# Gathering the second expert table by used experts, with four places for tiles and three for rows

## The chip, the cores and the metric

The kernel runs on one core of one Trainium2 chip. The metric is the device time of the whole program in microseconds (us). TensorE is the matrix engine, VectorE (DVE) and ScalarE (ACT) the elementwise ones, GpSimd (POOL) issues the indirect DMAs through the software queue, SyncE (SP) issues the plain DMAs through a hardware queue.

## What is computed

A trunk of two layers over 256 tokens of width 2048. Each layer has four parallel mixers (Fourier, S5, attention, RWKV-7), a projection, and then a product-key expert layer ("PEER"). Only the last matters here, cut to its core:

```python
def peer_ffn(h, w_query, sub_keys, expert_u, expert_v):   # 8 heads, 128 x 128 = 16384 experts, top 16 a head
    q = (xc @ w_query).reshape(PEER_CHUNK, PEER_HEADS, 2, PEER_HALF)
    sc = jnp.einsum('chpd,hpkd->chpk', q, sub_keys)
    s1, i1 = lax.top_k(sc[:, :, 0], PEER_TOPK)
    s2, i2 = lax.top_k(sc[:, :, 1], PEER_TOPK)
    ...
    top_s, pos = lax.top_k(cand_s, PEER_TOPK)
    idx = jnp.take_along_axis(cand_i, pos, axis=-1)
    gate = jax.nn.softmax(top_s, axis=-1)
    u = jnp.take(expert_u, idx, axis=0)
    act = jax.nn.gelu(jnp.einsum('chkd,cd->chk', u, xc), approximate=False)
    vsel = jnp.take(expert_v, idx, axis=0)
    return jnp.einsum('chk,chkd->cd', (gate * act), vsel)
```

Each token picks 8 x 16 = 128 experts of 16384; each expert has one row of 2048 floats (8 KB) in each of two tables, `peer_u` and `peer_v`. All is float32.

## The kernel before

`build` runs a loop over the two layers; each iteration runs `mixers`, `rwkv`, `route` and `experts`. The change lies in `experts`, and in what `build` hands to it.

`experts` splits the 256 tokens. The first 160 (`DENSE`) go through the tables as a whole, in tiles: tile i holds the 128 experts with first key i, 1 MB. In the first stage TensorE multiplies each tile of the first table with the tokens (`tile(j)`, 16 products of 128x128 by 128x160, L1674, 32 matmul records), ScalarE applies GELU into `W[:, j, :]`. From tile `FIRST` = 64 on, `one_hot` and `gates` build, in 40 groups of 4 tokens, the matrix of gate weights by expert (L1683), and VectorE multiplies it into `W` (L1992 for tiles that are done, L1995 for the current one). After tile 127 `W[e, i, n]` is, for each of the 16384 experts and 160 tokens, gate times GELU, and it is exactly 0 where token n didn't pick the expert. In the second stage TensorE multiplies each tile of the second table by `W[:, j, :]` into six banks that hold the sum over all 128 tiles (L1747).

The other 96 tokens go by rows, in three sets of 32 (`SETS`). A "row" is one step: for 128 pairs of token and pick (one a partition) the row of the table is gathered. 32 steps on the first table give dot products, 32 on the second a weighted sum, so a layer has 192 row steps (`ROWS_IN`). GpSimd issues two gathers a step, one for each half of the row (L1631, 4 KB pieces for 128 partitions), into `place`, a ring of `RING` = 4 places, after `place_free` says that the step `RING` before is served. `serve(n)` on VectorE waits for the step's own DMA semaphore and runs one operation of 128x2048 (L1937 for the first table, L1943 for the second, L1940 for the first step of a sum). `served(j)` says how many steps stand in VectorE's order before tile j is over: 30 up to tile 63, then nine for ten tiles, 87 at tile 127; the other 105 follow freely during the second stage. The widened tokens of a set (`widen`, four groups of four transposes, L1697), and the folds of a set's sum into the output (`fold`, four single products, L1710, then `fold_add` on VectorE) stand at fixed tiles of TensorE's order: `WIDEN_0`, `WIDEN_1`, `FOLD_0` in the first stage, `WIDEN_2` = 36 and `FOLD_1` = 80 in the second. The third fold comes after the last tile.

Table tiles go through `ring`, `SLOTS` = 3 places of 1 MB. SP issues all 256 tile loads of a layer in order, each after `tile_mm` says that the tile `SLOTS` before it is multiplied (L1595 for the first table, L1600 for the second). TensorE waits on a semaphore of the place, `tile_in[slot]`. All orders are written by hand; nothing is planned at run time.

## Time and profile before

| | |
|---|---|
| median of three runs | 4014.94 us (4009.41 to 4017.21) |
| the profiled execution's own time | 4015.24 us |
| its span, first to last instruction | 4013.4 us |
| mean granted TensorE clock | 0.974 of full speed |
| TensorE busy (matmul / weight load) | 94% / 85% |
| VectorE, ScalarE, GpSimd busy | 57%, 11%, 24% |
| bytes moved by DMA | 1077.47 MB |

The expert part of a layer takes some 1200 us: in the first layer from 778 to 1986 us of the span, in the second from 2778 to 3988 us. A row of the profile has the line, engine, operation, what it writes and reads, how many, the busy time with the mean of one, and the idle time of the engine before it with what ended that. Matmul records overlap, since matmuls are pipelined, so a group's length counts and not the duration of one.

### The profile page before, as it was taken

The numbers are of one execution on the slowest core, as the hardware profiler recorded it, in microseconds if no ns is written. First come the engines' busy times: TensorE is split into PE (matmuls) and PEld (weight loads), VectorE is DVE, ScalarE is ACT, GpSimd is POOL, SyncE is SP. The second block draws the span as 40 slices with busy tenths as digits, with TensorE's granted clock in tenths as the row PEclk, the third lists the DMA queues.
The fourth block names the chain that finished last, engine by engine and source line by source line (L and its number), as shares of the span: only waits on it lengthen the run. The fifth ranks groups of instructions, "written<-read, shape, count | busy, mean of one in ns | idle before, by whom it ended". The sixth has DMA issues, their size and how long they took to land. (4 is left out here: it accounts for less than half of the span.)

```text
span 4013.4 us, 63920 instructions
## 1 busy us (share of the span) xinstructions
PE 3753.4 (94%) x26660; PEld 3401.8 (85%) x26660; DVE 2291.9 (57%) x4099; ACT 429.4 (11%) x1020; POOL 964.7 (24%) x868
## 2 busy tenths in 40 slices
PE   6997889999999999999879978899999999999997
PEld 5786774899999999999767867748999999999997
DVE  5965742785287544443469657517853875444434
ACT  1022210100111000000010232101001110000000
POOL 2610000034033333333225100000341333333331
PEclk9997899999999999999989978999999999999999
DMA  5430015399799999999744300154997999999997
GB/s 156 136 116 10 2 43 162 126 372 401 290 384 382 415 415 415 414 413 414 305 133 130 116 10 1 43 162 142 379 404 288 382 385 415 415 415 415 413 413 302
DMA packets 334770, 1077.47 MB, mean 268 GB/s; under 512 B 52196, under 2 KB 150872, under 8 KB 268440
## 3 DMA queue, kind: packets, MB, share of 16 engines
q1 hardware_dynamic: 223896, 670.72, 44.0%
q0 software_dynamic: 110592, 402.70, 25.3%
q8 instruction: 212, 3.47, 0.4%
q14 instruction: 70, 0.57, 0.0%
HBM read 1071.23 MB, written 2.10 MB: 267 GB/s over the span
## 5 line engine op out<-in xcount | busy, mean ns | idle before, releaser
L1747 PE MATMUL bank<-ex_W,ex_tile 128*128 128x160 f32 x8192 | 1132.3, 300 | 38.8 <-DMA ex_tile<-in_peer_v 38.8
L1747 PEld LDWEIGHTS bank<-ex_W,ex_tile 128*128 128x128 f32 x8192 | 1114.9, 190 | 59.7 <-DMA ex_tile<-in_peer_v 53.0
L1674 PE MATMUL bank<-ycT,ex_tile 128*128 128x160 f32 x8192 | 1140.2, 300 | 20.3 <-DMA ex_tile<-in_peer_uT 19.9
L1674 PEld LDWEIGHTS bank<-ycT,ex_tile 128*128 128x128 f32 x8192 | 1116.9, 190 | 36.0 <-DMA ex_tile<-in_peer_uT 30.4
L1631 POOL DMA_INDIRECT ex_row<-in_peer_u,ex_rows x384 | 403.5, 1051 | 1852.7 <-DVE ex_rows L1907 1187.4
L1943 DVE SCALAR_TENSOR_TENSOR ex_sums<-ex_row,ex_weight,ex_sums 128x2048 f32<-128x2048 f32 x186 | 436.9, 2349 | 412.9 <-DMA ex_row<-in_peer_v,ex_rows 412.8
L1937 DVE CUSTOM_DVE_ANT_0 ex_row<-ex_row,ex_h_wide 128x2048 f32<-128x2048 f32 x192 | 438.5, 2290 | 363.7 <-DMA ex_row<-in_peer_u,ex_rows 362.4
L1631 POOL DMA_INDIRECT ex_row<-in_peer_v,ex_rows x384 | 363.7, 947 | 878.9 <-DVE ex_sums L1943 565.7
L359 PE MATMUL pj_bank<-pj_hT,pj_piece 128*128 128x256 f32 x2048 | 458.7, 383 | 5.6 <-DMA pj_piece<-in_w_in 3.8
L359 PEld LDWEIGHTS pj_bank<-pj_hT,pj_piece 128*128 128x128 f32 x2048 | 387.9, 191 | 71.5 <-issue 13.8
L826 PE MATMUL bank<-arena,ycT 128*128 128x512 f32 x512 | 222.4, 593 | 2.0 <-PEq L911 2.0
L826 PEld LDWEIGHTS bank<-arena,ycT 128*128 128x128 f32 x512 | 96.6, 190 | 121.4 <-issue 121.2
L996 PE MATMUL bank<-arena 128*128 128x128 f32 x1152 | 140.7, 283 | 7.6 <-DVE arena L1344 7.5
L996 PEld LDWEIGHTS bank<-arena 128*128 128x128 f32 x1152 | 136.5, 198 | 10.3 <-issue 10.1
L1995 DVE TENSOR_TENSOR ex_W<-ex_W,ex_gelu 128x160 f32<-128x160 f32 (+26 forms) x128 | 35.2, 275 | 182.2 <-ACT ex_gelu L1791 113.8
L1419 PE MATMUL bank<-ycT,query_w 128*128 128x256 f32 x512 | 114.9, 382 | 2.0 <-PEq L1436 2.0
L1793 ACT ACTIVATE ex_W<-bank 128x160 f32<-128x160 f32 (+20 forms) x206 | 56.9, 276 | 518.4 <-PE bank L1674 518.4
L1419 PEld LDWEIGHTS bank<-ycT,query_w 128*128 128x128 f32 x512 | 95.8, 190 | 16.5 <-issue 2.7
L1921 DVE TENSOR_SCALAR ex_hot<-consts,ex_picksT 128x128 f32<-128x128 f32 x320 | 109.1, 341 | 0.0
L1518 DVE TENSOR_TENSOR x<-bank,x 128x512 f32<-128x512 f32 x16 | 11.1, 692 | 168.3 <-PE bank L826 168.1
L1920 DVE TENSOR_SCALAR ex_hot<-consts,ex_picksT 128x128 f32<-128x128 f32 x320 | 90.1, 282 | 15.4 <-ACT ex_picksT L1825 15.4
L607 POOL TENSOR_TENSOR s_table<-s_factor 128x1024 f32<-128x1024 f32 x16 | 30.8, 1927 | 268.7 <-DVE s_factor L712 153.1
(375 smaller groups left out, 3107.0 us busy)
## 6 DMA issues: line engine op xcount, KB each, us to landing
ex_tile<-in_peer_uT SPq DMA_DIRECT2D x256, 1024.0 KB, 8.1
ex_tile<-in_peer_v SPq DMA_DIRECT2D x256, 1024.0 KB, 8.2
pj_piece<-in_w_in SPq DMA_DIRECT2D x32, 2048.0 KB, 8.8
arena<-in_w_out SPq DMA_DIRECT2D x16, 2048.0 KB, 8.1
query_w<-in_peer_w_query SPq DMA_DIRECT2D x16, 1024.0 KB, 5.8
ex_row<-in_peer_u,ex_rows POOLq DMA_INDIRECT x384, 13.0
ex_row<-in_peer_v,ex_rows POOLq DMA_INDIRECT x384, 12.4
x<-in_x SPq DMA_DIRECT2D x1, 2048.0 KB, 8.9
```

What stands on the lines that cost most here:

```text
L359: mm = mmul(pj_bank[:, n % 2, m * SEQ:m * SEQ + SEQ], piece[:, n % 2, k, m * P:m * P + P], hT[:, k, :], start=(m == 0 and k == 0), stop=(k ...
L826: mm = nc.tensor.matmul(bank[:, out_bank(n) + b, :], ycT[:, kh * HALF_K + k, b * P:b * P + P], out_w["place"][:, i % 2, k, :], start=(kh = ...
L996: mm = mmul(bank[:, b, j * P:j * P + P], left[:, d, j, :], right[:, d, j, :], start=(j == 0), stop=True, skip_group_check=True)
L1419: mm = nc.tensor.matmul(bank[:, h % 2, 0:SEQ], query["w"][:, h % WRING, k, :], hT[k // 4][:, k % 4, :], start=(k == 0), stop=(k == KT - 1) ...
L1631: nc.gpsimd.indirect_dma_start(out=place[:, n % RING, half * D // 2:(half + 1) * D // 2], out_offset=None, in_=tables[table][:, :], in_off ...
L1674: mm = mmul(o, ring[:, j % SLOTS, k * P:k * P + P], hT[k // 4][:, k % 4, 0:DENSE], start=(k == 0), stop=(k == KT - 1))
L1747: mm = mmul(bank[:, at_, lo:lo + DENSE], ring[:, i % SLOTS, m * P:m * P + P], W[:, j, :], start=(j == 0 and m % 3 == 0), stop=(j == TILES ...
L1793: last = A.activation(W[:, j, n:DENSE], a[:, n:DENSE], ACT.Gelu)
L1920: V.tensor_scalar(hot2[:, g % 2, i, :], c("iota"), picksT[:, 1, n:n + 1], None, ALU.is_equal)
L1921: mm = V.tensor_scalar(hot1[:, g % 2, i, :], c("iota"), picksT[:, 0, n:n + 1], picksT[:, 2, n:n + 1], ALU.is_equal, ALU.mult)
L1937: V.tensor_tensor_reduce(out=row, in0=row, in1=h_wide[:], scale=1.0, scalar=0.0, op0=ALU.mult, op1=ALU.add, accum_out=dot[:, step:step + 1 ...
L1943: V.scalar_tensor_tensor(sums[:], row, weight[:, step:step + 1], sums[:], ALU.mult, ALU.add)\
```

## The change

The tiles of the second table are no longer loaded whole by SP. VectorE works out an index for each expert (`want`, for eight tiles at a time, `CHUNK`): the largest absolute value of `W` over the 160 tokens, a comparison with 0 that gives 65536 where it is 0, and an addition of the expert's number (`expert`: key times 128 plus partition plus the layer's base). GpSimd issues one indirect gather a tile (`v_tile`), 128 indices, 8 KB pieces; an index beyond the last expert is out of bounds and is skipped, so the place keeps what it had, which is multiplied by a `W` of 0. The first 13 chunks' indices are made in VectorE's order after tiles 104 to 116, the last three after tile 127. GpSimd's order is now written out: rows up to `rows_ahead(0)` = 86, then for each tile of the second table its gather and, until the 192 are out, one row step (two gathers). The ring of tiles has four places, that of rows three. TensorE waits for a second-table tile on a new semaphore a place, `v_in`, whose value goes on over the layers, so it is compared with a value that depends on the layer. The fixed tiles of `widen(2)` and `fold(1)` move from 36 to 28 and from 80 to 64, and the row before which `fold_add(1)` starts from 152 to 149.

```diff
--- before.py
+++ after.py
@@ -33,8 +33,8 @@
 HALF_K = 8
 WRING = 3
 TILES = KEYS
-SLOTS = 3
-RING = 4
+SLOTS = 4
+RING = 3
 SET, SETS, STEPS = 32, 3, 32
 DENSE = SEQ - SET * SETS
 ROWS_IN = SETS * 2 * STEPS
@@ -43,7 +43,7 @@
 FIRST = 64
 BEFORE = 30
 WIDEN_0, EXPS_1, WIDEN_1, FOLD_0 = 2, 16, 90, 114
-WIDEN_2, FOLD_1, FOLD_1_AT = 36, 80, 152
+WIDEN_2, FOLD_1, FOLD_1_AT = 28, 64, 149
 A_BANKS = (4, 5, 3)
 G_BANKS = (0, 1, 2)
 OUT_BANKS = (0, 1, 2, 3, 4, 5)
@@ -92,6 +92,7 @@
     parts["fold"] = (p % SET) == np.arange(SET)[None, :]
     parts["even"] = (p // S5C) % 2 == 0
     parts["odd"] = (p // S5C) % 2 == 1
+    parts["lane"] = p
     parts["eps"] = np.full((P, 1), NORM_EPS)
     parts["eps_kk"] = np.full((P, 1), 1e-12)
     parts["eps_gn"] = np.full((P, 1), 64e-5)
@@ -167,6 +168,7 @@
 
 
         row_in = [sem(f"row_in{i}") for i in range(RING)]
+        v_in = [sem(f"v_in{i}") for i in range(SLOTS)]
         kept = len(first_sem)
         with nc.Fori(0, DEPTH) as layer:
             rw = ExitStack()
@@ -193,7 +195,7 @@
                      "rms": sb(rw, "rms", [P, 3, TB]), "w_in": [sem(f"query_in{i}") for i in range(WRING)]}
             hT = [ycT[:, 4 * g:4 * g + 4] for g in range(4)]
             route(nc, t, layer, sem, sb, bank, c, col, x, ycT, hT, query, out_w)
-            experts(nc, t, layer, sem, sb, bank, c, x, hT, query, W, low, layer_base, row_in)
+            experts(nc, t, layer, sem, sb, bank, c, x, hT, query, W, low, layer_base, row_in, v_in)
             rw.close()
             with nc.Block() as block:
                 @block.sync
@@ -1524,12 +1526,24 @@
                 do(V.reciprocal(rms[:, 2], rms[:, 1]))
 
 
+NOWHERE = 65536.0
+CHUNK = 8
+
+
+def rows_ahead(j):
+
+    return min(served(TILES - SLOTS - 1) + RING - 1 + j, ROWS_IN)
+
+
 def served(j):
 
     return BEFORE + max(j - FIRST + 1, 0) * 9 // 10
 
 
-def experts(nc, t, layer, sem, sb, bank, c, x, hT, query, W, low, layer_base, row_in):
+def experts(nc, t, layer, sem, sb, bank, c, x, hT, query, W, low, layer_base, row_in, v_in):
+
+
+
 
 
 
@@ -1546,6 +1560,7 @@
                                                                                       "gates_times", "tile_times")]
     four_ready, rows_ready, place_free, dots_ready, gelu_ready, sums_ready = [sem("ex_" + n) for n in ("four", "rows", "place_free", "dots",
                                                                                           "gelu", "sums")]
+    index_ready = sem("ex_index")
     wide_mm, wide_out, fold_mm, fold_added = [sem("ex_" + n) for n in ("wide_mm", "wide_out", "fold_mm", "fold_added")]
     out_mm, out_out, back_mm, x_added, dve_own = [sem("ex_" + n) for n in ("out_mm", "out_out", "back_mm", "x_added", "dve")]
     with ExitStack() as st:
@@ -1566,6 +1581,8 @@
         picksT = sb(st, "ex_picksT", [P, 3, DENSE])
         rows = sb(st, "ex_rows", [P, SETS, 2, STEPS], U32)
         half_on = sb(st, "ex_half_on", [P, 1])
+        weighty, expert = sb(st, "ex_weighty", [P, TILES]), sb(st, "ex_expert", [P, TILES])
+        wanted = sb(st, "ex_wanted", [P, TILES], U32)
         share_w = sb(st, "ex_share", [P, SETS, STEPS])
         dot, dot_gelu = sb(st, "ex_dot", [P, STEPS]), sb(st, "ex_dot_gelu", [P, STEPS])
         weight = sb(st, "ex_weight", [P, STEPS])
@@ -1585,6 +1602,7 @@
         best = nc.alloc_sbuf_tensor_at("ex_best", [P, TB, PEER_H, TOPK], F32, offset=before_hot + 3072)
         outT = W[:, 0:KT, :]
         tables = [t[n].rearrange("l e (h d) -> (l e h) d", h=2) for n in ("peer_u", "peer_v")]
+        v_rows = t["peer_v"].rearrange("l e d -> (l e) d")
 
         with nc.Block() as block:
             @block.sync
@@ -1593,11 +1611,6 @@
                     if free is not None:
                         sp.wait_ge(tile_mm, free)
                     sp.dma_start(ring[:, slot, :], t["peer_uT"][layer, i].rearrange("p k e -> p (k e)"))\
-                        .then_inc(tile_in[slot], 16)
-
-                def v_tile(i, slot, free):
-                    sp.wait_ge(tile_mm, free)
-                    sp.dma_start(ring[:, slot, :], t["peer_v"].rearrange("l (i e) d -> l i e d", e=KEYS)[layer, i])\
                         .then_inc(tile_in[slot], 16)
 
                 for h in range(WRING, PEER_H):
@@ -1611,19 +1624,10 @@
                         u_tile(lap * SLOTS + e, e, lap * SLOTS + (e + 1 - SLOTS))
                 for i in range(whole_laps * SLOTS, TILES):
                     u_tile(i, i % SLOTS, i + 1 - SLOTS)
-                ahead = SLOTS - TILES % SLOTS
-                for i in range(ahead):
-                    v_tile(i, (TILES + i) % SLOTS, TILES + i + 1 - SLOTS)
-                with sp.Fori(0, (TILES - ahead) // SLOTS) as lap:
-                    for e in range(SLOTS):
-                        v_tile(lap * SLOTS + (ahead + e), e, lap * SLOTS + (TILES + ahead + e + 1 - SLOTS))
-                for i in range(ahead + (TILES - ahead) // SLOTS * SLOTS, TILES):
-                    v_tile(i, (TILES + i) % SLOTS, TILES + i + 1 - SLOTS)
 
             @block.gpsimd
             def _(pool):
-                pool.wait_ge(rows_ready, SETS * 4 * 2)
-                for n in range(ROWS_IN):
+                def gather(n):
                     s, table, step = n // (2 * STEPS), n // STEPS % 2, n % STEPS
                     if n >= RING:
                         pool.wait_ge(place_free, n - RING + 1)
@@ -1633,6 +1637,24 @@
                             in_=tables[table][:, :],
                             in_offset=bass.IndirectOffsetOnAxis(ap=rows[:, s, half, step:step + 1], axis=0))\
                             .then_inc(row_in[n % RING], 16)
+
+                def v_tile(j):
+                    slot = (TILES + j) % SLOTS
+                    if j % CHUNK == 0:
+                        pool.wait_ge(index_ready, j // CHUNK + 1)
+                    pool.wait_ge(tile_mm, TILES + j + 1 - SLOTS)
+                    nc.gpsimd.indirect_dma_start(
+                        out=ring[:, slot, :], out_offset=None, in_=v_rows[:, :],
+                        in_offset=bass.IndirectOffsetOnAxis(ap=wanted[:, j:j + 1], axis=0),
+                        bounds_check=DEPTH * EXPERTS - 1, oob_is_err=False).then_inc(v_in[slot], 16)
+
+                pool.wait_ge(rows_ready, SETS * 4 * 2)
+                for n in range(rows_ahead(0)):
+                    gather(n)
+                for j in range(TILES):
+                    v_tile(j)
+                    for n in range(rows_ahead(j), rows_ahead(j + 1)):
+                        gather(n)
 
             @block.tensor
             def _(pe):
@@ -1733,7 +1755,7 @@
                 pe.wait_ge(gates_times, GROUPS)
                 for j in range(TILES):
                     i = TILES + j
-                    pe.wait_ge(tile_in[i % SLOTS], 16 * (i // SLOTS + 1))
+                    pe.wait_ge(v_in[i % SLOTS], layer * (16 * ((TILES - 1 - j % SLOTS) // SLOTS + 1)) + 16 * (j // SLOTS + 1))
                     if j >= FIRST:
                         pe.wait_ge(tile_times, j - FIRST + 1)
                     if 0 <= j - WIDEN_2 < 4:
@@ -1922,6 +1944,15 @@
                                              picksT[:, 2, n:n + 1], ALU.is_equal, ALU.mult)
                     mm.then_inc(hot_ready, 1)
 
+                def want(i):
+
+                    some = slice(CHUNK * i, CHUNK * i + CHUNK)
+                    dve.wait_ge(gates_times, GROUPS)
+                    dve.wait_ge(tile_times, max(CHUNK * i + CHUNK - FIRST, 1))
+                    do(V.tensor_reduce(weighty[:, some], W[:, some, :], AX.X, ALU.max, apply_absolute_value=True))
+                    do(V.tensor_scalar(weighty[:, some], weighty[:, some], 0.0, NOWHERE, ALU.is_equal, ALU.mult))
+                    V.tensor_tensor(wanted[:, some], weighty[:, some], expert[:, some], ALU.add).then_inc(index_ready, 1)
+
                 def serve(n):
                     s, table, step = n // (2 * STEPS), n // STEPS % 2, n % STEPS
                     row = place[:, n % RING, :]
@@ -1976,6 +2007,9 @@
                     serve(n)
                 share(0)
 
+                do(V.tensor_scalar(expert[:], c("iota"), float(KEYS), c("lane"), ALU.mult, ALU.add))
+                do(V.tensor_scalar(expert[:], expert[:], layer_base[:], None, ALU.add))
+
                 dve.wait_ge(picks_out, 1)
                 one_hot(0)
                 one_hot(1)
@@ -1997,6 +2031,10 @@
                         one_hot(g + 2)
                     for n in range(served(j - 1), served(j)):
                         serve(n)
+                    if 0 <= g - GROUPS < (FIRST + GROUPS) // CHUNK:
+                        want(g - GROUPS)
+                for i in range((FIRST + GROUPS) // CHUNK, TILES // CHUNK):
+                    want(i)
                 for n in range(served(TILES - 1), ROWS_IN):
                     if n - FOLD_1_AT in (0, 2, 4, 6):
                         fold_add(1, (n - FOLD_1_AT) // 2)
```

## Rows read from the trace of the kernel before

**Rows 1.** The page, parts 1 and 2: busy time; GB/s in 40 slices.
```profile
PE 3753.4 (94%) x26660; PEld 3401.8 (85%) x26660; DVE 2291.9 (57%) x4099; ACT 429.4 (11%) x1020; POOL 964.7 (24%) x868
...
GB/s 156 136 116 10 2 43 162 126 372 401 290 384 382 415 415 415 414 413 414 305 133 130 116 10 1 43 162 142 379 404 288 382 385 415 415 415 415 413 413 302
```

**Rows 2.** Stages: us, PE, PEld, DVE, ACT, POOL busy, PEclk, DMA share, GB/s.
```profile
778.20:1060.60 282.40, 274.95 (x2002) 271.76 (x2001) 171.16 (x461) 30.77 (x78) 81.18 (x68) 1.00 0.90 354
1061.85:1276.20 214.35, 214.35 (x1637) 214.35 (x1637) 172.87 (x433) 31.61 (x127) 61.90 (x66) 1.00 0.93 356
1282.00:1394.66 112.66, 110.20 (x778) 105.09 (x777) 56.95 (x70) 7.29 (x24) 39.33 (x42) 1.00 1.02 414
1394.66:1986.10 591.44, 571.06 (x4122) 559.47 (x4120) 247.87 (x155) 7.61 (x16) 195.95 (x205) 1.00 1.01 410
3396.30:3987.70 591.40, 570.34 (x4116) 558.68 (x4114) 248.09 (x155) 7.22 (x15) 195.51 (x205) 1.00 1.01 410
```

**Rows 3.** TensorE in order of time: start us, us, what [idle before, releaser].
```profile
787.00 0.60 PE L1697 MATMUL bank<-consts,ex_four 128*128 128x128 f32 x4
787.43 4.51 PE L1674 MATMUL bank<-ycT,ex_tile 128*128 128x160 f32 x32
791.78 0.60 PE L1697 MATMUL bank<-consts,ex_four 128*128 128x128 f32 x4
...
1276.75 1.05 PE L1683 MATMUL bank<-ex_hot 128*128 128x128 f32 x8
1277.64 2.61 PE L1674 MATMUL bank<-ycT,ex_tile 128*128 128x160 f32 x18
...
1772.69 1.04 PE L1710 MATMUL bank<-ex_sums,consts 128*32 128x512 f32 x2
1773.67 2.58 PE L1747 MATMUL bank<-ex_W,ex_tile 128*128 128x160 f32 x17
```

**Rows 4.** The page, costliest groups: TensorE's tile products, busy and idle before.
```profile
L1747 PE MATMUL bank<-ex_W,ex_tile 128*128 128x160 f32 x8192 | 1132.3, 300 | 38.8 <-DMA ex_tile<-in_peer_v 38.8
...
L1674 PE MATMUL bank<-ycT,ex_tile 128*128 128x160 f32 x8192 | 1140.2, 300 | 20.3 <-DMA ex_tile<-in_peer_uT 19.9
```

**Rows 5.** Tile loads, issue to landing: u-tiles of 800 to 1000, v-tiles of 1400 to 1980.
```profile
DMA to landing us min/median/max: 4.7/8.2/9.8
...
DMA to landing us min/median/max: 7.8/8.2/9.5
```

**Rows 6.** Row gathers, to landing: 800 to 1000, 1100 to 1270, 1276 to 1394, 1400 to 1980.
```profile
DMA to landing us min/median/max: 4.5/11.2/19.4
...
DMA to landing us min/median/max: 6.8/8.1/11.4
...
DMA to landing us min/median/max: 6.3/12.2/18.2
...
DMA to landing us min/median/max: 8.7/15.7/21.8
```

**Rows 7.** GpSimd in order of time, v-stage: the two gathers of one row step.
```profile
1402.31 0.94 POOL L1631 DMA_INDIRECT ex_row<-in_peer_u,ex_rows  x1 [2.12 <-DVE ex_dot L1937]
1403.55 0.94 POOL L1631 DMA_INDIRECT ex_row<-in_peer_u,ex_rows  x1 [0.30 <-issue]
```

**Rows 8.** VectorE in order of time; then a reduction's group (busy us, mean ns).
```profile
1300.58 0.32 DVE L1995 TENSOR_TENSOR ex_W<-ex_W,ex_gelu 128x160 f32<-128x160 f32 x1 [1.81 <-ACT ex_gelu L1791]
...
1457.31 2.35 DVE L1943 SCALAR_TENSOR_TENSOR ex_sums<-ex_row,ex_weight,ex_sums 128x2048 f32<-128x2048 f32 x1 [5.63 <-DMA ex_row<-in_peer_v,ex_rows]
...
1981.80 4.85 DVE L1943 SCALAR_TENSOR_TENSOR ex_sums<-ex_row,ex_weight,ex_sums 128x2048 f32<-128x2048 f32 x2 [2.60 <-DMA ex_row<-in_peer_v,ex_rows]
...
L1882 DVE TENSOR_REDUCE ex_picks<-ex_match 128x32 f32<-128x512 f32 x32 | 21.9, 686 | 1.1
```

**Rows 9.** Waits of 778 to 1060.6: total us, times, longest.
```profile
DVE ex_row L1937 <- DMA ex_row<-in_peer_u,ex_rows: 49.4, 14, 6.9
DVE ex_total L1892 <- ACT ex_picks L1798: 48.0, 1, 48.0
```

## The prediction

> **What bounds the kernel now.** I read the page's first two parts, then the busy time by stage, then TensorE's order of time, then landings and waits. TensorE is busy for 94% of the span, and through the expert part of each layer DMA moves 380 to 415 GB/s in most slices [rows 1]. So two limits lie close together, and the stages must be priced one by one [rows 2]. I name them by table tile: "u-tiles" are the 128 of the first table, "v-tiles" the 128 of the second.
>
> TensorE's own pace [rows 3]: a tile is 32 matmul records; one starts at 787.43 and the group behind it at 791.78, so a tile is 4.35 us (the record of 4.51 holds the last matmul's tail, 0.16 us). A fold matmul adds 0.98 us (1773.67 - 1772.69), a group of four widening transposes 0.43 us (787.43 - 787.00), a gate group 0.89 us (1277.64 - 1276.75).
>
> Without any stall the stages of one layer would be:
> - u-tiles 0 to 61, 778.20 to 1060.60: 62 x 4.35 + 4 x 0.43 = 271.5 us, measured 282.4: 10.9 us of stall.
> - u-tiles 62 to 103 with the gates: 42 x 4.35 + 40 x 0.89 + 4 x 0.43 + 1.3 for the picks' transposes = 221.4 us; from 1060.60 to the end of tile 103 (1277.64 + 4.35 = 1282.0) it took 221.4. TensorE alone sets it.
> - u-tiles 104 to 127, 1282.00 to 1394.66: 24 x 4.35 + 4 x 0.98 = 108.3, measured 112.7: 4.4 us of stall.
> - v-tiles, 1394.66 to 1986.10: 128 x 4.35 + 4 x 0.98 + 4 x 0.43 = 563, measured 591.4, and 591.4 again in the second layer: 28 us of stall.
>
> The stalls end with an ex_tile transfer: 38.8 us of idle TensorE before v-tiles and 20.3 before u-tiles over both layers [rows 4] (the row counts less than I do, since each stall also lays bare a tail). In the v-stage DMA is at 410 GB/s. One MB-unit (1.05 MB, a full tile or a row pair for 128 partitions) at 410 to 415 GB/s costs 2.53 to 2.56 us, and 128 tiles plus 105 rows are 233 units, 590 to 596 us: the v-stage is exactly DMA-bound. Everything that the change can give there is 28 us a layer, not the time of the bytes it saves.
>
> **Part 1: bytes.** Which experts are used follows from the reference on its own inputs: I ran its top-k and marked, for the first 160 tokens (those that go through tiles), each expert that is picked. It leaves 11323 of 16384 in layer 0 (69.1%) and 11254 in layer 1 (68.7%), 53 to 118 of 128 in a tile. Skipping the rest saves 0.31 x 128 = 40 units a layer, 101 us of DMA time; the load falls to 193 units, 491 us. The average is under TensorE's 563 us.
>
> **Part 2: pacing.** The new program issues one row gather behind each v-tile until all 192 are out: 86 are out before the first v-tile, so 106 v-tiles carry a row, and 22 carry none. While rows run, a tile period asks 1.69 units, 4.27 to 4.33 us, against 4.35: 98% of TensorE's pace. This is an average over engines and tiles. A tile lands only when its slowest DMA engine is done. Taking eight partitions for an engine, the busiest eight (of consecutive ones) hold 75% in layer 0 and 73% in layer 1. Summed over windows of tiles, with the larger of 4.35 and the busiest eight's time at 2.53 us a unit, the mean period is 4.89 us if nothing evens out, 4.64 for windows of four tiles, 4.55 for eight, 4.47 for sixteen. There are four places for tiles and three for rows, so four to eight is what can even out; I take 4.6. The v-stage is then 106 x 4.6 + 22 x 4.35 = 583, and 2 us for that part of folds and widening that falls where TensorE is the later one: 585, 6 us less than 591.4. Ends: 563 (all hidden, -28) and, at 4.89, 614 + 6 = 620 (+29).
>
> The Trainium skill ("DMA: Bandwidth & Descriptors", The descriptor swizzle) gives the eight partitions of an engine in another order than mine, 0 to 3 with 32 to 35 and so on. Counted so, the busiest engine of layer 0 holds 78% of its rows and windows of four and eight give 4.63 and 4.55; the sum is the same by either, and no row here shows which engine serves which partition.
>
> **Part 3: GpSimd.** SP's v-tile loads, with nothing behind them on SP's queue, become gathers. A gather of 128 pieces takes 0.94 us and the next starts 1.24 us after it [rows 7]. Three a period are 3.72 us, within 4.6. A tile's pieces are 8 KB where rows' are 4 KB, and no row shows the cost of such an instruction: between 0.94 (one index, one piece; I take it, as the row is of 128 indices too) and twice that, 4.66 us a period. The queue is in order: v-tile j waits for tile j-4 to be multiplied, and the row gather behind it for its place; whichever waits holds the other. For the v-tile the cover is three tiles, 13.1 us.
>
> **Part 4: three row places.** A place's cycle is: second half issued 1.24 us after the first, landing, served in 2.35 us, 0.3 us to GpSimd's restart [rows 6, 7, 8]. At a landing of 8.1 us (gate stretch, DMA 93% busy) that is 12.0 us, 4.0 a row; at 15.7 us (v-stage of before, saturated) 19.6 us, 6.5 a row. At the 4.6 us I take, landing may be 9.9 us; I hold that it is near the 8.1 row, since 1.69 units in 4.6 us are 93% busy too. In the u-stage the gates stretch needs a row per 5.8 us: hidden. For tiles 104 to 127, landing 12.2 us gives 5.4 us a row, times 0.9 rows a tile 4.8 us a tile, against 4.7 now: 0 to 2 us a layer. Before tile 60 VectorE waits 49.4 us for rows and then 48.0 us for the softmax's exponentials [rows 9], which ScalarE makes only at tile 60: 30 rows, each 1.3 us later ((11.2 + 3.9) x (1/3 - 1/4) us, from the median landing there [rows 6]), use 38 us of that 48. Cost 0.
>
> **Part 5: four tile places.** A u-tile lands 8.2 us after issue, up to 9.8 [rows 5], and three places cover two tiles, 8.7 us: that is where the 10.9 us of stall come from, while DMA is at 90%. Four places cover 13.1 us, beyond every landing seen. I give back 9 of 10.9 us, bounds 0 and 10.9. In tiles 104 to 127 one more tile is there when the stretch begins and the first v-tile is only 0.69 units: DMA work falls from 44 units (22 u-tiles, a v-tile, 21 rows) to 42 (20, 0.69, 21), 106 us and under the 108.3. I take 3 of 4.4 us, bounds 0 and 4.4, and 1 us back for rows and for the next part.
>
> **Part 6: the index work.** Per 8 tiles one reduction of 128x1280 and two tiny operations. A 128x512 reduction takes 0.686 us [rows 8], so 1280 elements take at most 2.5 times that, 1.7, and the two others no more than the 0.32 of a 128x160 product each: 2.3 us at most, 16 times. The first 13 stand in tiles 104 to 116, where VectorE idles 1.81 us or more before each product [rows 8]; the serving and the product of the next tile are queued behind them. Cost 0 to 2 us, in the 1 us above. The last three run before v-tile 104 needs them. TensorE's waits now compare with a layer-dependent value: 0 to 0.07 us a tile, two serves back to back with such a wait take 4.85 us where each takes 2.35 [rows 8], 0.07 beside each; taken 0, since matmuls run unbroken over the present waits.
>
> **Sum.** Per layer -6 (v-stage) - 9 - 3 + 1 (u-stage) = -17, twice -34. The profiled execution had 4015.24 us (span 4013.4 and 1.8 around it), 0.3 from the median 4014.94. Forecast 4015 - 34 = 3981 us.
>
> **Rivals.** (a) The row and tile chains even out fully and the v-stage nears TensorE's floor: period 4.4 to 4.5, v-stage -17 to -28, total 3937 to 3962. For it: average demand 98%. Against: a tile with over 92 used experts asks, with its row, more than 4.35 us, and 49 and 53 of 128 in the two layers have more.
>
> (b) Slower: the shared queue. Now the v-tile lands in 8.2 us while a row beside it needs 15.7 [rows 5, 6]: a tile on SP's queue has a lead over what GpSimd's queue holds. In the new kernel v-tile and rows stand in GpSimd's queue, so the tile loses that lead, and three places for rows throttle GpSimd, which then issues the next v-tile late. It decides from a period of (602 - 98) / 106 = 4.75 us, where the v-stage loses the 11 us that the u-stage gives. At 4.9 us, a row landing of 10.8: v-stage 617, total 4015 + 2 x (26 - 11) = 4045. A doubled issue cost of the tile gathers (4.66 us and waits) ends there too. The Trainium skill ("DMA: Bandwidth & Descriptors", Queues, rings and completion order) says an engine takes turns between rings by packet; the landings above agree with it.
>
> (c) The skip saves nothing (an index beyond the bound still moves a piece): 2 units a period, 5.06 us, v-stage 106 x 5.06 + 98 = 634, total 4015 + 2 x (43 - 11) = 4079.
>
> (d) The gains and (b) cancel: period 4.7 to 4.8, 4007 to 4023.
>
> **Chances.** Forecast (3962 to 4006) 0.44, (a) 0.15, (d) 0.15, (b) 0.20 (4023 to 4070), (c) 0.06. Faster by over 0.2% (8 us, about what a measurement tells from no change) 0.59, within 0.15, slower 0.26. Range 3945 to 4050: it cuts the tips of (a) and (b), and (c).
>
> **What would show it.** Right: the bytes read fall by 80 units, 84 MB, the v-stage is 575 to 590 us, landings of rows there near 10 us, idle before u-tiles falls from 20 us to under 5. Wrong: GpSimd's v-tile gathers take near 2 us; bytes not lower; TensorE's wait for v-tiles grows; VectorE waits more before rows in tiles 104 to 127. The weakest step is the period of 4.6 us: 0.1 us there is 21 us in the total.

## The result, and the profile after

The changed kernel takes 4116.31 us (median of 4 runs, 4106.81 to 4123.07), the kernel before 4016.07 beside it: ratio 1.0251, 95% interval 1.0226 to 1.0275. It is 2.5% slower. The forecast, 3981 us in a range up to 4050, was wrong, in sign too. The profiled execution of after has 4114.04 us, span 4112.2.

The page of after, parts 1 and 2 (answering [rows 1]), then groups of its part 5 (answering [rows 4, 7]; in each, after the bar: busy time and mean ns of one, then the idle time before them and its releaser):

```profile
PE 3786.5 (92%) x26660; PEld 3428.7 (83%) x26660; DVE 2350.2 (57%) x4199; ACT 429.4 (10%) x1020; POOL 1501.8 (37%) x1124
GB/s 152 133 113 10 1 61 140 186 391 414 311 383 390 337 337 336 347 341 328 131 129 129 113 10 1 63 140 204 393 412 310 374 389 357 341 337 343 337 320 125
DMA packets 334774, 994.07 MB, mean 242 GB/s; under 512 B 62385, under 2 KB 161061, under 8 KB 278629
...
L1769 PE MATMUL bank<-ex_W,ex_tile 128*128 128x160 f32 x8192 | 1170.3, 305 | 111.1 <-DMA ex_tile<-in_peer_v,ex_wanted 110.1
...
L1696 PE MATMUL bank<-ycT,ex_tile 128*128 128x160 f32 x8192 | 1132.3, 300 | 0.0
...
L1635 POOL DMA_INDIRECT ex_row<-in_peer_v,ex_rows x384 | 471.8, 1229 | 435.5 <-DVE ex_sums L1974 207.2
...
L1646 POOL DMA_INDIRECT ex_tile<-in_peer_v,ex_wanted x256 | 377.3, 1474 | 194.4 <-PE bank L1769 128.2
```

Three things stand here. The bytes fell as worked out. The idle time before u-tiles is gone (20.3 us before). The idle time before v-tiles went from 38.8 to 111.1 us although DMA there moves only some 340 GB/s, and the mean of GpSimd's gathers, 1.23 and 1.47 us, is no longer near the 0.94 on which the sum rested. (A gather is one indirect DMA that GpSimd issues; its mean is GpSimd's busy time for one.)

By stages, for both kernels (us, layer 1 / layer 2; the stages are those of [rows 2]):

| | u-tiles 0–61 | 62–103 | 104–127 | v-stage |
|---|---|---|---|---|
| before | 282.4 / 282.6 | 221.4 | 112.7 / 113.1 | 591.5 / 592.3 |
| forecast | 273.4 | 221.4 | 110.7 | 585 |
| after | 271.4 / 271.3 | 221.4 | 118.6 / 116.2 | 648.4 / 648.6 |

The spans differ by 98.8 us: v-stages +56.9 +56.3, early u-tiles -11.0 -11.3, late u-tiles +5.9 +3.1, and 1 less in the rest. (Some expectations below count 645 us for this stage, or a period of 5.14 us; the stages of the table give 648.5 and 5.19.) Busy time of each engine by stretch in after (columns: stretch and length, PE, PEld, DVE, ACT, POOL, each with its count, then the granted clock, DMA's busy share and GB/s): tiles 104 to 127, the v-stage of layer 1, that part of it in which rows run, the v-stage of layer 2.

```profile
1271.90:1390.60 118.70, 111.04 (x779) 106.14 (x778) 79.62 (x109) 7.29 (x24) 40.97 (x41) 0.97 0.96 378
1390.60:2039.00 648.40, 590.75 (x4122) 572.05 (x4122) 253.84 (x164) 7.65 (x16) 468.33 (x336) 0.98 0.87 313
1390.60:1935.00 544.40, 487.25 (x3365) 469.20 (x3365) 249.14 (x162) 5.17 (x11) 444.79 (x315) 0.98 0.93 338
3438.90:4087.50 648.60, 590.18 (x4123) 571.92 (x4122) 253.57 (x164) 7.60 (x16) 468.75 (x336) 0.98 0.86 312
```

In the 544.4 us with rows GpSimd is busy for 444.79 in 315 gathers, and each gather has 0.30 us ahead of it: 445 + 95 = 540 us. GpSimd has no time left. TensorE is busy for only 487 us of the stretch, and DMA moves 338 GB/s where before it moved 410. GpSimd's order of time in after, and below it VectorE's over the same microseconds (start, duration, engine, line, operation; in brackets the idle time before it and its releaser):

```profile
1501.40 1.00 POOL L1646 DMA_INDIRECT ex_tile<-in_peer_v,ex_wanted  x1 [0.30 <-issue]
1502.70 0.94 POOL L1635 DMA_INDIRECT ex_row<-in_peer_v,ex_rows  x1 [0.30 <-issue]
1503.94 2.38 POOL L1635 DMA_INDIRECT ex_row<-in_peer_v,ex_rows  x1 [0.30 <-issue]
1506.63 0.99 POOL L1646 DMA_INDIRECT ex_tile<-in_peer_v,ex_wanted  x1 [0.31 <-issue]
1507.93 1.85 POOL L1635 DMA_INDIRECT ex_row<-in_peer_v,ex_rows  x1 [0.30 <-issue]
1510.08 0.94 POOL L1635 DMA_INDIRECT ex_row<-in_peer_v,ex_rows  x1 [0.30 <-issue]
1511.33 3.11 POOL L1646 DMA_INDIRECT ex_tile<-in_peer_v,ex_wanted  x1 [0.31 <-issue]
```
```profile
1503.16 2.35 DVE L1974 SCALAR_TENSOR_TENSOR ex_sums<-ex_row,ex_weight,ex_sums 128x2048 f32<-128x2048 f32 x1 [4.12 <-DMA ex_row<-in_peer_v,ex_rows]
1506.61 2.35 DVE L1974 SCALAR_TENSOR_TENSOR ex_sums<-ex_row,ex_weight,ex_sums 128x2048 f32<-128x2048 f32 x1 [1.10 <-DMA ex_row<-in_peer_v,ex_rows]
1511.21 2.35 DVE L1974 SCALAR_TENSOR_TENSOR ex_sums<-ex_row,ex_weight,ex_sums 128x2048 f32<-128x2048 f32 x1 [2.25 <-DMA ex_row<-in_peer_v,ex_rows]
```

A tile gather takes 1.00 us, not 1.88, so the larger pieces are not the cost. But a gather that begins while VectorE passes over a row ends 0.8 to 0.9 us after that pass: 1505.51 + 0.81 = 1506.32, 1508.96 + 0.82 = 1509.78, 1513.56 + 0.88 = 1514.44. It happens to row and tile gathers alike. Below this is called the hold. The gather at 1506.63 isn't held: it begins 0.02 us behind the start of its pass, so what starts first seems to go first. Between 1400 and 1900 us there are 289 gathers, three for each of 96 v-tiles. Of these 105 begin inside a pass. Ten of the 105 begin in the first 0.1 us of it and take their usual time, and 95 are held and take 2.36 us on average. The 184 that begin outside a pass take 0.94 (median). One in three, 1.4 us longer: 3 x 1.26 + 1.4 x 95 / 96 = 5.17 us a v-tile, against 500 / 96 = 5.2 measured.

### The profile page after: what moved, and what is told of

Read it like the earlier page. It is cut to its first block and busy times, and to the rows that moved or that the text cites. A ratio compares the mean times of both kernels' runs of the same rounds, so it can differ in the third digit from the quotient of the medians.

```text
span 4112.2 us, 63500 instructions
## 1 busy us (share of the span) xinstructions
PE 3786.5 (92%) x26660; PEld 3428.7 (83%) x26660; DVE 2350.2 (57%) x4199; ACT 429.4 (10%) x1020; POOL 1501.8 (37%) x1124
## 5 line engine op out<-in xcount | busy, mean ns | idle before, releaser
L1769 PE MATMUL bank<-ex_W,ex_tile 128*128 128x160 f32 x8192 | 1170.3, 305 | 111.1 <-DMA ex_tile<-in_peer_v,ex_wanted 110.1
L1769 PEld LDWEIGHTS bank<-ex_W,ex_tile 128*128 128x128 f32 x8192 | 1139.9, 193 | 144.9 <-DMA ex_tile<-in_peer_v,ex_wanted 137.0
L1635 POOL DMA_INDIRECT ex_row<-in_peer_u,ex_rows x384 | 455.4, 1186 | 1669.2 <-DVE ex_rows L1929 1187.6
L1635 POOL DMA_INDIRECT ex_row<-in_peer_v,ex_rows x384 | 471.8, 1229 | 435.5 <-DVE ex_sums L1974 207.2
L1646 POOL DMA_INDIRECT ex_tile<-in_peer_v,ex_wanted x256 | 377.3, 1474 | 194.4 <-PE bank L1769 128.2
L1983 DVE TENSOR_TENSOR x<-bank,x 32x512 f32<-32x512 f32 x24 | 16.6, 690 | 239.8 <-PE bank L1732 239.5
L1421 PE MATMUL bank<-ycT,query_w 128*128 128x256 f32 x512 | 114.9, 382 | 2.0 <-PEq L1438 2.0
L1943 DVE TENSOR_SCALAR ex_hot<-consts,ex_picksT 128x128 f32<-128x128 f32 x320 | 109.9, 343 | 0.0
L1815 ACT ACTIVATE ex_W<-bank 128x160 f32<-128x160 f32 (+20 forms) x206 | 56.9, 276 | 496.1 <-PE bank L1696 496.1
```

Source lines behind the costliest of these rows:

```text
L1421: mm = nc.tensor.matmul(bank[:, h % 2, 0:SEQ], query["w"][:, h % WRING, k, :], hT[k // 4][:, k % 4, :], start=(k == 0), stop=(k == KT - 1) ...
L1635: nc.gpsimd.indirect_dma_start(out=place[:, n % RING, half * D // 2:(half + 1) * D // 2], out_offset=None, in_=tables[table][:, :], in_off ...
L1646: nc.gpsimd.indirect_dma_start(out=ring[:, slot, :], out_offset=None, in_=v_rows[:, :], in_offset=bass.IndirectOffsetOnAxis(ap=wanted[:, j ...
L1769: mm = mmul(bank[:, at_, lo:lo + DENSE], ring[:, i % SLOTS, m * P:m * P + P], W[:, j, :], start=(j == 0 and m % 3 == 0), stop=(j == TILES ...
L1815: last = A.activation(W[:, j, n:DENSE], a[:, n:DENSE], ACT.Gelu)
L1943: mm = V.tensor_scalar(hot1[:, g % 2, i, :], c("iota"), picksT[:, 0, n:n + 1], picksT[:, 2, n:n + 1], ALU.is_equal, ALU.mult)
```

## Experiments

The theories weighed: the hold (a VectorE pass keeps GpSimd's gather from going on, so GpSimd sets the period), the bytes or the shared software queue (tile and rows delay each other while they land), the three row places, and the number of gathers. In the ratios each kernel stands against the kernel before in runs taken beside it. "Period" is (v-stage - 98) / 106, as in the prediction: the time from one v-tile to the next while rows run, with 98 us taken off for the 22 tiles without a row and for folds and widening. After has 5.19 in both layers.

**Passes with one input.** On the changed kernel, both row operations read the row alone, in nearly the same time, and the 96 tokens that go by rows get no expert output:

```diff
-    V.tensor_tensor_reduce(out=row, in0=row, in1=h_wide[:], scale=1.0, scalar=0.0, op0=ALU.mult, ...)
+    V.tensor_reduce(dot[:, step:step + 1], row, AX.X, ALU.max).then_inc(place_free, 1)
-    V.scalar_tensor_tensor(sums[:], row, weight[:, step:step + 1], sums[:], ALU.mult, ALU.add) ...
+    V.tensor_reduce(sums[:, step:step + 1], row, AX.X, ALU.max).then_inc(place_free, 1)
```

> The changed kernel, but VectorE serves a row by a maximum along the row (one input from SBUF, about as long, 2.29 us) in place of the dot product and of the scaled addition (two inputs from SBUF). Which part is left out: the 96 tokens that go by rows get no expert output of their own. Theory L (a gather that starts while VectorE runs a pass with two SBUF inputs is held until that pass ends): no gather of the second-table stage above 1.1 us, a tile period of 4.4 to 4.7 us in place of 5.14, that stage 570 to 595 us in place of 648, total 3950 to 3995 us. Theory Q (the software queue itself holds the gathers: too many pieces outstanding, or the tiles' 8 KB pieces): gathers of 2 to 3 us stay, one in three, the stage stays at 640 to 655 us, total 4100 to 4125.

Measured: 4019.92 us against 4021.91, ratio 0.9997 (0.9988 to 1.0007); v-stages 601.3 / 602.3, period 4.75. GpSimd and then VectorE in this kernel, and the window of its rows:

```profile
1500.05 1.00 POOL L1646 DMA_INDIRECT ex_tile<-in_peer_v,ex_wanted  x1 [0.30 <-issue]
1501.35 0.94 POOL L1635 DMA_INDIRECT ex_row<-in_peer_v,ex_rows  x1 [0.30 <-issue]
1502.60 0.94 POOL L1635 DMA_INDIRECT ex_row<-in_peer_v,ex_rows  x1 [0.31 <-issue]
1505.64 1.00 POOL L1646 DMA_INDIRECT ex_tile<-in_peer_v,ex_wanted  x1 [2.11 <-remote]
```
```profile
1500.57 2.29 DVE L1973 TENSOR_REDUCE ex_sums<-ex_row 128x1 f32<-128x2048 f32 x1 [2.10 <-DMA ex_row<-in_peer_v,ex_rows]
```
```profile
1386.50:1890.00 503.50, 480.69 (x3403) 467.70 (x3403) 248.39 (x122) 5.17 (x11) 302.88 (x316) 0.99 0.98 372
```

The gather at 1501.35 begins inside a pass of 2.29 us and takes 0.94. VectorE is as busy as in after (248.39 us against 249.14), but GpSimd's 316 gathers fall from 445 to 303 us. Of 162 that begin inside a reduction's pass between 1400 and 1900 us none is held, so the hold doesn't come from VectorE being busy. Without it the change is worth nothing and costs nothing. That is less than the expectation had: the stage and the total both lie above its ranges. A second cost is left, seen in the 2.11 us before the tile gather at 1505.64.

These reductions also write one number a partition where the passes that they replace write 2048, so this kernel alone doesn't say which of the two matters. Two pairs of rows in after do; in each the VectorE pass comes first, then the gather that begins inside it:

```profile
1735.12 0.69 DVE L1983 TENSOR_TENSOR x<-bank,x 32x512 f32<-32x512 f32 x1 [4.74 <-PE bank L1732]
1735.27 0.93 POOL L1635 DMA_INDIRECT ex_row<-in_peer_u,ex_rows  x1 [0.30 <-issue]
```
```profile
1445.61 1.35 DVE L1971 TENSOR_SCALAR ex_sums<-ex_row,ex_weight 128x2048 f32<-128x2048 f32 x1 [1.24 <-DMA ex_row<-in_peer_v,ex_rows]
1446.24 1.52 POOL L1635 DMA_INDIRECT ex_row<-in_peer_v,ex_rows  x1 [0.30 <-issue]
```

The first pass writes as much as it reads, but one of its inputs (`bank`) lies in PSUM and only `x` in SBUF. The gather in it isn't held; it ends 0.39 us after the pass. So writing alone doesn't hold a gather. The second pass is the first step of a sum. It reads one large tensor and one number a partition, in 1.35 us where a reduction of as many elements takes 2.29, and it does hold the gather, which ends 0.80 us after it. Three gathers of the kernel with one-input passes are held in the same way, all inside this operation, which that kernel keeps. So a pass with two large inputs in SBUF holds a gather, and so does this faster pass with one; there are only three of the latter in a layer.

**The same arithmetic in two short passes.** The scaled addition of the second table is split at column 1024.

```diff
-    V.scalar_tensor_tensor(sums[:], row, weight[:, step:step + 1], sums[:], ALU.mult, ALU.add) ...
+    V.scalar_tensor_tensor(sums[:, 0:1024], row[:, 0:1024], weight[:, step:step + 1], sums[:, 0:1024], ...)
+    V.scalar_tensor_tensor(sums[:, 1024:2048], row[:, 1024:2048], weight[:, step:step + 1], ...)
```

> The changed kernel, but the scaled addition of the second table's rows is two passes of 1024 elements in place of one of 2048. The dot products of the first table's rows stay one pass of 2048. Same result. Theory L (a gather that begins inside a two-input pass ends 0.82 us behind that pass): if the two halves let GpSimd in between, held gathers take at most 1.2 + 0.8 = 2.0 us while second-table rows are served, and up to 3.1 while first-table rows are; stage 610 to 640 us. If the second half takes the port at once, held gathers are as long as before and the stage stays at 640 to 650. Theory Q (the queue holds them): no difference between the two kinds of rows.

Measured: 4015.76 us, ratio 1.0014 (1.0005 to 1.0024), v-stages 603.8 / 601.2: nearly all of the 2.5% is back, with no gather and no byte less, and the stage is shorter than the 610 to 640 us expected. GpSimd and VectorE in this kernel:

```profile
1515.51 1.89 POOL L1635 DMA_INDIRECT ex_row<-in_peer_v,ex_rows  x1 [0.30 <-issue]
```
```profile
1515.30 1.29 DVE L1974 SCALAR_TENSOR_TENSOR ex_sums<-ex_row,ex_weight,ex_sums 128x1024 f32<-128x1024 f32 x1 [2.26 <-DMA ex_row<-in_peer_v,ex_rows]
1516.50 1.28 DVE L1976 SCALAR_TENSOR_TENSOR ex_sums<-ex_row,ex_weight,ex_sums 128x1024 f32<-128x1024 f32 x1
```

The gather is held by the first half alone: 1516.59 + 0.81 = 1517.40, though the second half begins at once. So the hold lasts for one instruction, and half the pass is half the hold: gathers that begin at least 0.1 us inside a scaled addition take 1.49 us on average here, and 2.40 in after.

**Bytes, with GpSimd full and with it free.** On the changed kernel every expert is gathered again (`NOWHERE` replaced by 0.0 in `want`):

> The changed kernel, but no expert is counted as unused, so every tile of the second table is gathered whole, by the same instructions. Theory L: GpSimd sets the period (5.14 us) and a whole tile with its row needs 5.06 us of DMA, so little changes: stage 645 to 675 us, total 4105 to 4170. Theory Q: 31% more tile pieces in the same queue, GpSimd held longer for each: stage over 690 us, total over 4200. A third theory (D: the saved bytes are what the stage lives on): 31% of 128 units, 40 x 2.53 = 101 us a layer more, total over 4300.

Measured: 4095.68 us, ratio 1.0192 (1.0175 to 1.0209), 1077.50 MB, v-stages 640.7 / 638.8. That is no slower than after: 83 MB more cost nothing. It is even 0.6% faster by the two ratios, and below the range expected; why is open. The saved bytes lie idle beside a full GpSimd. The same edit on the kernel with whole-row gathers (next paragraph), where GpSimd is not full:

> Whole-row gathers, and no expert counted as unused. With GpSimd out of the way the saved bytes should count: two full units a period, 5.06 us, so the second-table stage is 106 x 5.06 + 98 = 634 us against 571 for whole-row gathers alone; total 4070 to 4095. If the bytes don't matter here either, the total stays at 3960 to 3975.

Measured: 4073.62 us, ratio 1.0156 (1.0139 to 1.0172), v-stages 630.1 / 628.4 against 573.1 / 568.8 with the skip. Here the 83 MB are worth 57 and 60 us a layer, 3.1% of the whole by the two ratios. The skip does what it says; it only pays once GpSimd can keep up.

**One gather for a row instead of two.** On the changed kernel, 2 gathers a period for 3:

```diff
-    for half in range(2):
-        nc.gpsimd.indirect_dma_start(out=place[:, n % RING, half * D // 2:(half + 1) * D // 2], ...
-            in_offset=bass.IndirectOffsetOnAxis(ap=rows[:, s, half, step:step + 1], axis=0))
+    nc.gpsimd.indirect_dma_start(out=place[:, n % RING, :], ...
+        in_offset=bass.IndirectOffsetOnAxis(ap=rows[:, s, 0, step:step + 1], axis=0))
```

> The changed kernel, but a row step is one gather of 128 pieces of 8 KB in place of two of 4 KB. The result is the same. Theory L: two gathers a period, 2 x 1.24 + 1.4 us of being held = 3.9 us, under TensorE's 4.35, so GpSimd no longer sets the pace: period 4.4 to 4.7 us, stage 570 to 595, total 3950 to 3995. Theory Q: the same bytes in the same queue, in pieces of 8 KB only: stage 630 us or more, total 4080 or more.

Measured: 3959.2 us, ratio 0.9853 (0.9836 to 0.9869): faster than both kernels. From its windows, groups and GpSimd's order of time:

```profile
1387.80:1961.00 573.20, 567.84 (x4123) 559.51 (x4122) 253.04 (x164) 7.73 (x16) 298.72 (x229) 1.00 0.90 352
```
```profile
L1767 PE MATMUL bank<-ex_W,ex_tile 128*128 128x160 f32 x8192 | 1123.9, 300 | 8.5 <-DMA ex_tile<-in_peer_v,ex_wanted 8.0
```
```profile
1504.74 3.10 POOL L1644 DMA_INDIRECT ex_tile<-in_peer_v,ex_wanted  x1 [0.30 <-issue]
```

Gathers are still held for up to 3.1 us, but two of them, 1.24 and 1.30 us when unheld, leave 1.8 us of TensorE's 4.35 for the hold. The idle time before v-tiles falls from 111.1 to 8.5 us. Early u-tiles cost 277.7 / 279.1 instead of 271.4. With one-input passes on top, and with the split passes on top:

> One-input serving (as in the first experiment, so the 96 row tokens get no expert output) together with whole-row gathers. With one-input serving alone no gather was held, yet a tile period was still 4.74 us; with whole-row gathers alone, where gathers are held, it was 4.45. Theory P (what is left at 4.74 us is the rows coming as two gathers of 4 KB pieces, not the holding): period 4.4 to 4.5, second-table stage 563 to 575 us, total 3950 to 3962. Theory S (the one-input pass brings a cost of its own): period stays over 4.6, total 3985 or more.

> The changed kernel with whole-row gathers and the scaled addition in two passes. Same result. Whole rows alone gave 3959 us (ratio 0.985), with gathers held up to 3.1 us but a period of 4.45; with no gather held at all 3949. Theory L with slack: shorter holds are worth little once there are two gathers a period: 3948 to 3960.

Measured: 3948.71 us, ratio 0.9847 (0.983 to 0.9863), v-stages 569.2 / 564.8; and 3961.46, ratio 0.985 (0.9831 to 0.9868), v-stages 575.6 / 568.7. With two gathers a period the hold is worth 4 us a layer at most. The loss needs both, three gathers a period and long holds, and removing either takes most of it.

**What is left without holds: evenness, places or gathers.** One-input passes leave a period of 4.75 us where two gathers a period leave 4.45. The forecast's cause was unevenness over DMA engines. In this kernel (one-input passes, no index from `W`) every fourth partition is skipped in each tile instead, `parts["lane"] = p + 65536 * (p % 4 == 0)`:

> One-input serving with two gathers a row step, as in the first experiment (no gather held, second-table stage 601 us at 0.69 units a tile), but the rows that are skipped are the same fourth partition of every tile, whatever the token picks: 0.75 units a tile, the same for any eight partitions. Which part is left out: the 96 row tokens' expert output, and a quarter of the experts. Theory U (what is left is that a tile's load is uneven over the DMA engines and from tile to tile): more bytes but a shorter stage, a period of 4.43 to 4.5 us, 568 to 578 us, total 3955 to 3975. Theory P (the many 4 KB pieces or the longer cycle of a row place set the pace): the stage stays at 600 us or grows, total 4015 or more.

Measured: 4015.27 us, ratio 0.998 (0.997 to 0.999), v-stages 601.0 / 605.0 (in the slowest of its ten runs, 4026.76 us), as with the real, uneven experts. An even load was expected to bring 568 to 578 us at the 0.75 units a tile that it moves, so evenness is not it. Then three gathers again, with whole rows and the tile fetched in two halves of 4 KB (one-input passes):

```diff
-    nc.gpsimd.indirect_dma_start(out=ring[:, slot, :], ... ap=wanted[:, j:j + 1]
+    for half in range(2):
+        nc.gpsimd.indirect_dma_start(out=ring[:, slot, half * D // 2:(half + 1) * D // 2], ... ap=wanted[:, half, j:j + 1]
```

> One-input serving and whole-row gathers (period 4.45 us, 3949 us in all), but now the tile comes as two gathers of 4 KB pieces. So a period has three gathers again, as with one-input serving alone (4.74 us, 4020 us in all), while a row place's cycle stays short. Which part is left out: the 96 row tokens' expert output. Theory N (the number of gathers or of pieces in the software queue sets the 4.74 us): period over 4.65, stage 592 us or more, total over 3990. Theory C (the longer cycle of a row place does, by its second gather): period 4.4 to 4.5, total 3945 to 3965.

Measured: 4006.11 us, ratio 0.9959 (0.9945 to 0.9973), v-stages 594.2 / 595.0, period 4.68, where whole tiles gave 569.2 / 564.8. The row places turn as in the kernel with whole rows, so it is not their cycle; it is the third gather, or its 128 more pieces, and no kernel here tells these two apart. In this kernel, in the even one and in the one with one-input passes GpSimd stands idle before every third tile gather; GpSimd's waits in the last (us in total, times, longest):

```profile
POOL ex_tile L1646 <- PE bank L1769: 153.7, 54, 3.4
POOL ex_tile L1646 <- remote: 152.7, 66, 3.1
```

The 66 stops of "remote" have no releaser that the profile knows, and none stands in after, in the kernel with split passes or with two gathers a period. What ends them stays open.

**The places.** The kernel before with four places for tiles and three for rows (`SLOTS = 4`, `RING = 3`), nothing else:

> The kernel before with four places for tiles and three for rows, nothing else: the second table is still loaded whole by SP. Theory L (the loss is GpSimd's alone): first-table stage 15 us shorter a layer as in the changed kernel, second-table stage DMA-bound as before at 585 to 592 us, total 3975 to 3990. Rival R (three row places throttle the rows, in whichever kernel): rows end late, second-table stage over 600 us, total 4010 or more.

Measured: 4036.03 us, ratio 1.0043 (1.0029 to 1.0057). Early u-tiles 271.3 / 271.9, late ones 114.9 / 110.9, v-stages 587.4 / 589.4. The stages sum to 29 us less than before, and yet the kernel loses, behind the last v-tile of each layer; in layer 2:

```profile
4003.32 6.45 PE L1710 MATMUL bank<-ex_sums,consts 128*32 128x512 f32 x8 [21.16 <-DVEq L1947]
```

With SP's tiles one place further ahead and rows one fewer, the rows end some 21 us late, in either layer (from layer 1's last v-tile to layer 2's first u-tile it is 813.5 us against 792.4). So the stage came out as the first theory of the expectation had it, and the total as the rival had it, by a wait that stands outside the stage. The reverse check, whole rows on the changed kernel with three tile places and four for rows:

> The changed kernel with whole-row gathers, but with the places of before: three for tiles, four for rows. Same result. If the fourth tile place is what takes the first-table stalls away and covers the landings of about 10 us (three places cover 8.7 us), the first-table stage to tile 62 goes back to 282 us or more from 277, the second-table stage to 585 or more from 571, total over 3990. If the places don't matter with whole rows, the total stays at 3955 to 3965.

Measured: 4059.49 us, ratio 1.0093 (1.007 to 1.0116): early u-tiles 297.0 / 294.2, late ones 117.9 / 119.5, v-stages 592.7 / 599.3. Against whole rows with four and three places, the fourth tile place (and one row place fewer) is worth 15 to 19 us in early u-tiles, and 20 to 30 in the v-stage. Whole rows on the kernel before, where SP loads all tiles, and the same with four and three places:

> The kernel before (tiles of both tables loaded whole by SP, three tile places, four row places) with whole-row gathers, nothing else. If the gain of whole-row gathers comes only from GpSimd's load in the changed kernel, this changes nothing: 233 units are still 590 us, total 4010 to 4025. If 8 KB row pieces help on their own, by moving more bytes a second or by taking turns evenly with tile pieces, the total is under 4005; if they take DMA time away from the tiles, it is over 4030.

> The kernel before (SP loads both tables whole) with whole-row gathers and four tile places, three row places. Whole rows with three tile places gave 4127: tile landings of 9.1 to 10.2 us against a cover of 8.7. If that was the cover, four places (13.1 us) repair it: first-table stage to tile 62 at 271 to 278 us, second-table stage DMA-bound at 588 to 592 (233 units), total 3975 to 4005. If 8 KB row pieces cost the tiles in another way, the total stays over 4060.

Measured: 4126.88 us, ratio 1.028 (1.0263 to 1.0297), early u-tiles 297.2 / 293.1, v-stages 629.6 / 632.9; and 4064.79, ratio 1.0105 (1.0087 to 1.0123), early u-tiles 277.9 / 279.4, v-stages 623.4 / 623.7. The fourth place was right for the early u-tiles. The 588 to 592 us expected for the v-stage with four places, and the total, were missed. In the v-stage of the second of them:

```profile
1971.34 39.39 PE L1745 MATMUL bank<-ex_W,ex_tile 128*128 128x160 f32 x288 [1.73 <-DMA ex_tile<-in_peer_v]
```

Up to here every tile comes after a wait at a period near 5 us (4.97 between starts); once the rows are out, nine tiles run without one. So rows of 8 KB pieces take from SP's tiles a larger share than rows of 4 KB (with three tile places a v-tile lands in 10.2 us, median, where before it took 8.2). They run ahead and end early, and in the end DMA has tiles alone to fetch, 1.05 MB in TensorE's 4.35 us or 241 GB/s, while before it had both at its limit. In the kernel before rows and tiles end together: the last fold waits 0.64 us behind the last tile. That its pairs of 4 KB gathers keep them in step is argued from this, not shown. What pays when tiles and rows share GpSimd's queue costs when they don't: 2.8% with the places of before, and 0.6% with four and three (1.0105 against 1.0043).

**Rows spread out.** GpSimd's total work in the v-stage is what counts, not its rhythm: on the changed kernel seven row steps for eight tiles (`RING - 1 + j * 7 // 8`, and `FOLD_1_AT` 140), so that rows run beside 122 v-tiles, not 106:

> The changed kernel (two gathers a row step, two-input serving), but the 106 row steps of the second-table stage go behind 122 tiles, seven for eight tiles, in place of one for each of the first 106; the first row that a fold waits behind moves from 149 to 140. Same result. If GpSimd's time is what the stage costs while rows run and it lies idle in the last 22 tiles, the sum 106 x (2 x 1.24 + 1.39) + 128 x 1.30 = 577 us can spread over 563 us of TensorE's work: stage 577 to 605 us against 645, total 3980 to 4035. If the loss belongs to each row step, wherever it stands, nothing is gained: 4100 to 4120.

Measured: 4030.64 us, ratio 1.002 (1.0011 to 1.003), v-stages 605.6 / 607.9: 2.3 of the 2.5% back by order alone, with holds as before (2.35 us for a held gather, between 1400 and 1880 us). The stage is 1 to 3 us above the range expected. In after GpSimd had little to do beside the last 22 v-tiles. All three cures together (whole rows, split passes, spread rows):

> Whole-row gathers, the scaled addition in two passes and the rows spread over 122 tiles. Same result. Whole rows gave 3959 us with a period of 4.45; the spread asks 0.69 + 0.87 = 1.56 units a tile, 3.95 us of DMA, well under TensorE's 4.35. Theory L with slack: second-table stage 563 to 568 us against 571, total 3943 to 3956. If something else holds it, it stays at 3957 to 3965.

Measured: 3945.88 us, ratio 0.9814 (0.9797 to 0.983), the fastest of all, with nothing of the computation left out. Its v-stage and groups:

```profile
1388.80:1952.50 563.70, 563.31 (x4123) 558.79 (x4122) 261.50 (x226) 7.64 (x16) 285.51 (x230) 1.00 0.93 359
```
```profile
L1694 PE MATMUL bank<-ycT,ex_tile 128*128 128x160 f32 x8192 | 1139.0, 300 | 11.1 <-DMA ex_tile<-in_peer_uT 10.9
L1767 PE MATMUL bank<-ex_W,ex_tile 128*128 128x160 f32 x8192 | 1117.3, 299 | 0.6 <-DMA ex_tile<-in_peer_v,ex_wanted 0.5
```

563.7 us is within 1 us of the floor of 563 that the prediction had worked out for TensorE alone, and TensorE is busy for 563.31 of it.

## Why the prediction was wrong

**Part 3 failed, and it alone decides the sign.** The step is the price of a gather. It took a gather at 0.94 us from [rows 7], started 1.24 us apart, and 3.72 us a period as cover. The tile gather's size was right (1.00 us, lower bound). The price 0.94 came from rows in which VectorE stood still: in before a row gather waits for VectorE to free its place, so it starts when the pass has just ended, and between 1400 and 1880 us only 4 of 170 are held by a pass (they end 0.81 us after it). In after tile gathers run by TensorE's clock and push the row gathers out of step with the passes. The upper bound, a gather twice as long, was put on the wrong thing: it was for larger pieces, where the cost lies in what VectorE runs. A third of the gathers at 2.36 us make 5.17 us a period, 0.57 over the assumed 4.6: 106 x 0.57 = 60 us over the forecast's 585 in the v-stage, and 63 and 64 were measured.

The Trainium skill ("SBUF — State Buffer", Who interferes with whom) says that GpSimd and VectorE share a pair of ports, that a VectorE instruction with two SBUF inputs takes it against a GpSimd instruction that reads SBUF, for its whole length, and that one with at most one input does not, outside the 2-port modes, which `tensor_scalar` can enter. The gathers read their indices from SBUF and both row passes have two inputs. The traces agree: reductions and the pass with one input in PSUM hold nothing, and in the TENSOR_SCALAR pass with one large input, 1.35 us long, a gather takes 1.52 us in place of 0.94. The prediction didn't weigh it; by it 3.72 us was no safe cover.

**Part 2 was wrong in its cause.** It put 4.6 us down to DMA engines unevenly loaded. An even skip left 601 us as it was, and with GpSimd out of the way the uneven tiles run at 4.4 to 4.5 us a period, and at TensorE's 4.35 with rows spread. Less than half of the 22 us that Part 2 charged for it is left. Rival (a) named that, with its time of 3937 to 3962. Whole-row gathers land at 3959, but they are another kernel than the one that (a) spoke of.

**Part 1 was right**, 83.4 MB less where 84 were forecast, and rival (c) falls with it, though the 4079 that it gave lies nearer to the result than any other.

**Rival (b) had the side and the point of decision, not the mechanism.** Its threshold of 4.75 us held: the kernel with one-input passes has that period and comes out level. But it expected rows to land in 10.8 us and to throttle GpSimd. The landings between 1400 and 1900 us in after, rows and then tiles:

```profile
DMA to landing us min/median/max: 5.4/6.6/8.8
```
```profile
DMA to landing us min/median/max: 6.1/7.5/9.6
```

The medians are shorter than all of [rows 5, 6]. So the queue isn't where the time goes; what the gathers cost is paid on GpSimd. Its side remark, doubled issue cost with waits, was nearest, but was priced at the end of (b), 4045.

**Part 5 was right for early u-tiles**: 9 forecast, 11.0 and 11.3 measured, just over its upper bound of 10.9. **For late ones it was wrong**: -3 + 1 forecast, +5.9 and +3.1 measured. TensorE in after:

```profile
1321.98 4.61 PE L1696 MATMUL bank<-ycT,ex_tile 128*128 128x160 f32 x32
1334.26 1.88 PE L1732 MATMUL bank<-ex_sums,consts 128*32 128x512 f32 x2 [7.66 <-DVE x L1983]
1336.07 5.66 PE L1696 MATMUL bank<-ycT,ex_tile 128*128 128x160 f32 x32
```

It waits 7.66 us for VectorE to add a fold, and then a tile takes 5.66 us, not 4.61: from 1331.4 to 1338.2 the granted clock is 0.50. VectorE, just before:

```profile
1331.51 1.48 DVE L1952 TENSOR_REDUCE ex_weighty<-ex_W 128x8 f32<-128x1280 f32 x1
1333.02 0.17 DVE L1953 TENSOR_SCALAR ex_weighty<-ex_weighty 128x8 f32<-128x8 f32 x1
1333.23 0.17 DVE L1954 TENSOR_TENSOR ex_wanted<-ex_weighty,ex_expert 128x8 uint32<-128x8 f32 x1
1333.43 0.68 DVE L1983 TENSOR_TENSOR x<-bank,x 32x512 f32<-32x512 f32 x1
```

The index work costs 1.82 us, under its bound of 2.3. But Parts 4 and 6 shared one microsecond, each priced beside an idle VectorE. In this stage VectorE now also waits 26.3 us for rows (11 times, longest 4.4), where before it waited only for ScalarE's products, 55.7 us in 24 waits, and fold_add is queued behind both. The kernel with changed places and no index work has 114.9 / 110.9 here (before 112.7 / 113.1), with 33.3 us of row waits in layer 1: the places alone bring 2 us of lateness in layer 1 and none in layer 2. The kernel with whole rows has the same places and the index work, and takes 110.1 / 110.0. So it takes more than one of these together; what the index work adds was not run alone.

**The clock.** TensorE's 4122 records of the v-stage take 590.75 us busy in after and 571.06 in before, at granted clocks of 0.98 and 1.00. In each v-stage of after the granted clock falls seven times to its lower level (1.2 of 2.4 GHz), for 3.4 us each, every time behind a wait of 1.9 to 3.3 us; before has none. One such wait in layer 2, and the stretch behind it:

```profile
3552.32 9.96 PE L1769 MATMUL bank<-ex_W,ex_tile 128*128 128x160 f32 x59 [3.20 <-DMA ex_tile<-in_peer_v,ex_wanted]
```
```profile
3553.50:3556.90 3.40, 3.40 (x15) 3.40 (x14) 2.05 (x1) 0.00 (x0) 2.79 (x3) 0.50 1.03 414
```

At 4.35 us for 32 records, 59 take 8.2 us with their tail, and here they take 9.96. Seven times that is some 12 us a layer; the rest of the 20 is tails laid bare by the waits. The sum had no term for this. It is a consequence of the waits and not a cause of its own: with whole rows the clock is 1.00 again. How much of the 12 us reaches the stage, while GpSimd sets the period, isn't shown.

**Slips in the sums.** By its own terms TensorE's floor of the v-stage is 562.4 us, not 563, and that stage took 592.3 us in layer 2, not 591.4 again. With 11 us given back a layer, as at their other ends, (a) ends at 3959 and (d) begins at 4003, not 3962 and 4007. None of these moves the forecast.

## What to carry to other kernels

Take the price of a GpSimd gather from a stretch in which VectorE runs what it will run beside the new gathers; a gather that waits for a VectorE pass to end never meets that pass, and its row in the trace hides the hold. Before bytes are saved by moving loads to GpSimd, add up its gathers for a period with one held until a pass ends, and cut their number or the length of each pass first. And a balance between two DMA queues belongs to its piece size: with four tile and three row places whole-row gathers brought 3.9% behind one queue (ratio 1.0251 to 0.9853) and cost 0.6% behind two (1.0043 to 1.0105); behind two queues with three and four places they cost 2.8%.

## What the runs showed of the hardware

- An indirect gather of 128 pieces keeps GpSimd busy for 0.94 us when it fetches a row and 1.00 us when it fetches a v-tile under a bounds check; the next begins 0.30 us later. The size of a piece makes no difference: whole rows in pieces of 8 KB take 0.94 us too, and half tiles in pieces of 4 KB take 0.99 (rows of the kernels with whole rows and with tile halves; minimum, median and maximum in ns):

```profile
L1634 POOL DMA_INDIRECT ex_row<-in_peer_v,ex_rows x64: 932/936/945, 1424.0 to 1852.1; - x64
L1645 POOL DMA_INDIRECT ex_tile<-in_peer_v,ex_wanted x214: 984/990/1620, 1403.2 to 1899.1; - x107
```

- A gather begun more than 0.1 us inside a VectorE pass with two large SBUF inputs ends 0.81 us (median) after that pass. Inside a TENSOR_REDUCE of the same length, or a TENSOR_TENSOR with one of its inputs in PSUM, it takes its usual time. A TENSOR_SCALAR of 128x2048 with one large input holds it too.
- An index beyond the bound costs DMA nothing that shows: 994 MB for 1077, and 57 to 60 us a v-stage where bytes are the limit.
- Of two queues that share DMA, the one with 8 KB pieces gets ahead of where it was with 4 KB: early u-tiles went from 282 to 297 us in layer 1 and to 293 in layer 2 when rows' pieces grew from 4 to 8 KB, at the same bytes, and a u-tile's landing from 8.2 to 9.4 us (median).
- GpSimd's stops of 2 to 3 us with three unheld gathers a period remain unexplained.
